# Memory keys and values in three rounded passes, and the queries in the same block

## The reference, cut to what matters

```python
mem_k_p = mem_prompt @ xa_wk        # (256, 1024) @ (1024, 1024): keys of the memory, an output too
mem_v_p = mem_prompt @ xa_wv        # values of the memory, an output too
q = h @ xa_wq                       # (1056, 1024) @ (1024, 1024): queries
s = q @ k^T * 256**-0.5             # per head of 256
o = softmax(s) @ v
```

## Time and profile before

| what | us |
|---|---|
| median of three runs | 1609.36 (1607.07 to 1612.99) |
| the profiled execution | 1610.8 |
| its span, first to last instruction | 1608.8 |
| memory stage, first product to last (L2410) | 776.4 to 836.4 |
| queries, first pass to last | 844.0 to 939.3 |

### The profile page before, as it was taken

The page is one execution under the profiler, slowest core; times in us unless marked ns, Lnnn a source line. Parts: engine busy times, 40 slices in busy tenths (PEclk is TensorE's granted clock), DMA queues, the critical chain, the costliest instruction groups (busy, mean ns, idle before and its releaser), DMA issues. The chain is left out here.

```text
span 1608.8 us, 24942 instructions
## 1 busy us (share of the span) xinstructions
PE 1353.9 (84%) x9823; PEld 942.6 (59%) x9824; DVE 735.0 (46%) x1154; ACT 425.5 (26%) x897; POOL 189.1 (12%) x188
## 2 busy tenths in 40 slices
PE   5997999689987988799879989979951998999930
PEld 3665999655556886587439978768721333433310
DVE  4333464357755653676211013356545443444429
ACT  1213234168763321411111134332110111111110
POOL 0000000014327620000000000000000111111042
PEclk9998999789998995899899999989975999999975
DMA  9111121130003000300631025230074496792256
GB/s 330 45 54 40 40 55 50 38 90 17 1 4 120 4 4 15 134 1 1 235 105 40 14 105 211 104 138 1 1 288 172 147 352 221 287 338 78 74 164 216
DMA packets 79139, 174.32 MB, mean 108 GB/s; under 512 B 13076, under 2 KB 44955, under 8 KB 72627
## 3 DMA queue, kind: packets, MB, share of 16 engines
q1 hardware_dynamic: 69579, 137.73, 24.4%
q0 software_dynamic: 5856, 21.24, 4.3%
q10 hardware_dynamic: 3600, 13.90, 2.2%
HBM read 142.27 MB, written 30.66 MB: 107 GB/s over the span
## 5 line engine op out<-in xcount | busy, mean ns | idle before, releaser
L3071 PE MATMUL bank<-arena,hT 128*64 x384 | 172.9, 604 | 11.3 <-DVE hT L3180 4.9
L3072 PE MATMUL bank<-arena,hT 128*64 128x512 f32 x384 | 172.9, 604 | 0.0
L3071 PEld LDWEIGHTS bank<-arena,hT 128*64 128x64 f32 x384 | 53.3, 140 | 123.6 <-issue 123.6
L3191 DVE COPY arena<-arena 128x4096 f32 x24 | 55.1, 2295 | 130.3 <-PE bank L3072 118.3
L498 PE MATMUL bank<-arena,hT 128*128 128x344 f32 x384 | 114.4, 458 | 0.0
L498 PEld LDWEIGHTS bank<-arena,hT 128*128 128x128 f32 x384 | 73.5, 193 | 37.3 <-issue 1.4
L2146 PE MATMUL bank<-hT_rest,f_w_high 128*128 128x352 f32 x288 | 93.4, 324 | 0.0
L3039 POOL DMA_INDIRECT hT<-tokens,row_token x24 | 40.3, 1679 | 441.7 <-PE bank L3056 228.7
L3095 PE MATMUL bank<-arena,hT 128*64 x192 | 87.5, 599 | 2.4 <-ACT hT L3135 2.4
L3097 PE MATMUL bank<-arena,hT 128*64 128x512 f32 x192 | 87.5, 599 | 0.0
L1614 PE MATMUL bank<-arena 64*64 64x64 f32 (+1 forms) x1920 | 69.1, 224 | 3.5 <-DVE arena L1987 3.0
(11 more groups left out here) (490 smaller groups left out, 2946.7 us busy)
## 6 DMA issues: line engine op xcount, KB each, us to landing
arena<-in_ex_wg_dram SPq DMA_DIRECT2D x16, 1024.0 KB, 8.6
arena<-in_ex_wu_dram SPq DMA_DIRECT2D x16, 1024.0 KB, 10.9
arena<-in_ex_wd_dram SPq DMA_DIRECT2D x16, 1024.0 KB, 13.2
expert_rows<-hT ACTq DMA_DIRECT2D x24, 512.0 KB, 4.8
arena<-in_cache_mem_k_dram SPq DMA_DIRECT2D x8, 1024.0 KB, 5.0
arena<-in_w_in_dram SPq DMA_DIRECT2D x12, 512.0 KB, 4.0
h<-in_x_prompt_dram SPq DMA_DIRECT2D x8, 512.0 KB, 8.0
tokens<-h SPq DMA_DIRECT2D x8, 512.0 KB, 2.7
```

The costliest lines, as they stand in the source:

```text
L3071: nc.tensor.matmul(ps[UPB[u % 2]][0:LR, :], xT[:, u % 2, k, 0:LR], gate_up_of[:, bass.ds(slot, 1), :, k, :].rearrange("p a g f -> p (a g) ...
L3072: last = nc.tensor.matmul(ps[UPB[u % 2]][LR:P, :], xT[:, u % 2, k, LR:P], wB_gate_up[:, :, k, :], start=(k == 0), stop=(k == KC - 1))
L3191: nc.vector.tensor_copy(wB[:, 0:2 * EW], c.xw[:, bass.ds(e & 3, 1), 0:2 * EW].rearrange("p a n -> p (a n)")).then_inc(copied_up, 1)
```

## The change

`stage_memory` and `stage_queries` become one block, `stage_memory_and_queries`, so the engines no longer meet between them. The memory's products become `three_passes`: the turned memory is split into `memT_high` (ACT) and `memT_low` (DVE), and the weights come as eight pieces of 1 MB (512 columns of four `k`) in three slots; each piece is rounded by ACT into its own space and its rest is written by DVE over the raw piece. A piece `p` is loaded again into its slot when piece `p - 3` has been used (`done`). Each piece serves both groups of memory rows, so a bank's sum over eight `k` runs over two pieces. `load_memory_first` now loads `mem_prompt` and three pieces. SP issues the store of `Km` after the last piece's load and ahead of the query chunks, and the store of `Vm` behind the first four chunks; the waits for them stand at the end of the joint block, and a wait for the `Km` store stands on ACT ahead of the first copy into `qXT`.

```diff
 def place_memory(c):
     c.place(start=0, KT=KC * NMEM, Vm=2 * D, qXT=KC * TOK)
-    c.place(start=4096, Km=2 * D, mem=2 * D, memT=KC * NMEM, halves=3 * KC * 512)
+    c.place(start=2 * D, mem=2 * D)
+    c.place(start=4096, Km=2 * D, memTh=KC * NMEM, memTl=KC * NMEM, mR0=2048, mH0=2048, mR1=2048, mH1=2048, mR2=2048, mH2=2048)
+
+def load_memory_piece(c, sp, p):
+    src = c.T[('xa_wk', 'xa_wv')[p // 4]][0].rearrange("(k p) n -> p k n", p=P)
+    half, kh = p // 2 % 2, p % 2
+    n = (p + 2) % 3
+    sp.dma_start(c.A(f"mR{n}").rearrange("p (k n) -> p k n", k=4), src[:, 4 * kh:4 * kh + 4, half * 512:(half + 1) * 512])\
+        .then_inc(c.piece_in[n], 16)
 
 def load_memory_first(c, sp):
...
-    w = c.A("halves").rearrange("p (s k n) -> p s k n", s=3, k=KC)
-    sp.dma_start(w[:, 0], c.T['xa_wk'][0].rearrange("(k p) n -> p k n", p=P)[:, :, 0:512]).then_inc(c.half_in[0], 16)
+    for p in range(3):
+        load_memory_piece(c, sp, p)
...
         def _(sp):
-            for n in range(1, 4):
-                if n == 3:
-                    sp.wait_ge(prod, 2)
-                src = T[('xa_wk', 'xa_wv')[n // 2]][0].rearrange("(k p) n -> p k n", p=P)
-                sp.dma_start(w[:, n % 3], src[:, :, (n % 2) * 512:(n % 2 + 1) * 512]).then_inc(w_in[n % 3], 16)
-            sp.wait_ge(prod, 4)
-            for n in range(4):
-                load_query_chunk(c, sp, n)
-            for n, (name, t) in enumerate((('mem_k_prompt', Km), ('mem_v_prompt', Vm))):
-                sp.wait_ge(out_ok, 4 * (n + 1))
-                sp.dma_start(O[name][0, 0].rearrange("(m p) h d -> p m (h d)", p=P), t).then_inc(stored, 16)
-            sp.wait_ge(stored, 32)
+            for p in range(3, NP):
+                sp.wait_ge(done, p - 2)
+                load_memory_piece(c, sp, p)
+            sp.wait_ge(out_ok, 4)
+            sp.dma_start(O['mem_k_prompt'][0, 0].rearrange("(m p) h d -> p m (h d)", p=P), Km).then_inc(stored_k, 16)
+            sp.wait_ge(done, 6)
+            for n in range(4):
+                load_query_chunk(c, sp, n)
+            sp.wait_ge(out_ok, 8)
+            sp.dma_start(O['mem_v_prompt'][0, 0].rearrange("(m p) h d -> p m (h d)", p=P), Vm).then_inc(stored_v, 16)
+            for n in range(4, KC):
+                sp.wait_ge(q_prod, GRP * (n - 3))
+                load_query_chunk(c, sp, n)
+            sp.wait_ge(stored_k, 16)
+            sp.wait_ge(stored_v, 16)
 
         def _(pe):
-            pe.wait_ge(mT_ok, 4)
-            for u in range(8):
-                half, m = u // 2, u % 2
-                pe.wait_ge(w_in[half % 3], 16 * (half // 3 + 1))
-                if u >= 4:
-                    pe.wait_ge(out_ok, u - 3)
-                for k in range(KC):
-                    last = nc.tensor.matmul(ps[4 + u % 4][:, :], memT[:, k, m * P:(m + 1) * P], w[:, half % 3, k, :],
-                                            start=(k == 0), stop=(k == KC - 1))
+            def products(p):
+                half, kh = p // 2, p % 2
+                pe.wait_ge(wl_ok, p + 1)
+                if half >= 2 and kh == 0:
+                    pe.wait_ge(out_ok, 2 * (half - 1))
+                for m in range(2):
+                    for k in range(4):
+                        kk = 4 * kh + k
+                        if p < 2 and m == 0 and k % 2 == 0:
+                            pe.wait_ge(Tl_ok, kk // 2 + 1)
+                        t = slice(m * P, (m + 1) * P)
+                        last = three_passes(nc, ps[4 + 2 * (half % 2) + m][:, :], memT_high[:, kk, t], memT_low[:, kk, t],
+                                            w_high[slot(p)][:, k, :], w_low[slot(p)][:, k, :], kk == 0, kk == KC - 1)
+                last.then_inc(done, 1)
+            for p in range(NP):
+                products(p)
+                if p == 4:
+                    pe.wait_ge(out_ok, 4)
+                    for f in range(4):
+                        turns(Km, f, kturned)
+            pe.wait_ge(kT_ok, 4)
             for n in range(KC):
-                pe.wait_ge(low_ok, n + 1)
+                pe.wait_ge(ql_ok, n + 1)
...
         def _(act):
+            w_highs(0)
+            for f in range(4):
+                act.wait_ge(turned, f + 1)
+                nc.scalar.copy(memT_high[:, 2 * f:2 * f + 2, :], ps[f][:, :].rearrange("p (k m) -> p k m", k=2)).then_inc(Th_ok, 1)
+            for p in range(1, 6):
+                w_highs(p)
+            w_highs(6)
...
+            w_highs(7)
+            act.wait_ge(done, 7)
+            for n in range(3):
+                round_chunk(n)
+            act.wait_ge(stored_k, 16)
...
         def _(dve):
+            w_lows(0)
+            for f in range(4):
+                dve.wait_ge(Th_ok, f + 1)
+                nc.vector.tensor_tensor(memT_low[:, 2 * f:2 * f + 2, :], ps[f][:, :].rearrange("p (k m) -> p k m", k=2),
+                                        memT_high[:, 2 * f:2 * f + 2, :].bitcast(F32), ALU.subtract).then_inc(Tl_ok, 1)
+            for p in range(1, 3):
+                w_lows(p)
+            for half in range(3):
+                outs(half)
+                for p in (2 * half + 3, 2 * half + 4):
+                    if p < NP:
+                        w_lows(p)
+            for n in range(3):
+                chunk_low(n)
+            outs(3)
+            for n in range(3, KC):
+                chunk_low(n)
```

More of the change, by code:

```diff
@@ L2192, in stage_residual @@
         place_memory(c)
-        c.mem_in, c.half_in = s("mem"), [s(f"half{n}") for n in range(3)]
+        c.mem_in, c.piece_in = s("mem"), [s(f"piece{n}") for n in range(3)]
     w_in = c.w_out_in if split else [s(f"w{n}") for n in range(4)]
@@ L2435, in stage_queries @@
-def stage_queries(c):
-    nc, T = c.nc, c.T
+    fold = lambda x: x.rearrange("p (k m) -> p k m", k=KC)
+    memT_high, memT_low = fold(c.rounded("m_T_high", "memTh")), fold(c.rounded("m_T_low", "memTl"))
+    piece = lambda x: x.rearrange("p (k n) -> p k n", k=4)
+    w_raw = [piece(c.A(f"mR{n}")) for n in range(3)]
+    w_low = [piece(c.rounded(f"m_w_low{n}", f"mR{n}")) for n in range(3)]
+    w_high = [piece(c.rounded(f"m_w_high{n}", f"mH{n}")) for n in range(3)]
+    c.KT, c.Vm = KT, Vm
+    c.place(start=c.at["mR1"][0], qring=4 * KC * P, qhigh=4 * KC * P)
@@ L2443, in stage_queries, with slot @@
     ps = c.ps
-    s = lambda n: c.sem(f"q_{n}")
-    w_in, prod, evac, high_ok, low_ok = c.q_in, s("prod"), s("evac"), s("high"), s("low")
+    s = lambda n: c.sem(f"m_{n}")
+    mem_in, w_in = c.mem_in, c.piece_in
+    c.q_in = [s(f"q{n}") for n in range(4)]
+    turned, Th_ok, Tl_ok, wh_ok, wl_ok, done, out_ok, kturned, kT_ok, stored_k, stored_v = (
+        s("turned"), s("Th"), s("Tl"), s("wh"), s("wl"), s("done"), s("out"), s("kturned"), s("kT"), s("storedk"), s("storedv"))
+    q_prod, q_evac, qh_ok, ql_ok = s("qprod"), s("qevac"), s("qhigh"), s("qlow")
+    NP = 8
+    def slot(p):
+        return (p + 2) % 3
     with nc.Block() as block:
@@ L2464, in _, with w_highs, round_chunk @@
                                             c.hT_high[:, k, t], c.hT_low[:, k, t], k == 0, k == KC - 1)
-                    last.then_inc(prod, 1)
+                    last.then_inc(q_prod, 1)
+        @block.scalar
+        def _(act):
+            def w_highs(p):
+                act.wait_ge(w_in[slot(p)], 16 * (p // 3 + 1))
+                if p >= 3:
+                    act.wait_ge(done, p - 2)
+                nc.scalar.copy(w_high[slot(p)], w_raw[slot(p)]).then_inc(wh_ok, 1)
+            def round_chunk(n):
+                act.wait_ge(c.q_in[n % 4], 16 * (n // 4 + 1))
+                nc.scalar.copy(high[:, n % 4], ring[:, n % 4]).then_inc(qh_ok, 1)
+            w_highs(0)
[5 more added lines that the diff above has]
+            w_highs(6)
+            for f in range(4):
+                act.wait_ge(kturned, f + 1)
+                nc.scalar.copy(KT[:, 2 * f:2 * f + 2, :], ps[f][:, :].rearrange("p (k m) -> p k m", k=2)).then_inc(kT_ok, 1)
+            w_highs(7)
[3 more added lines that the diff above has]
+            act.wait_ge(stored_k, 16)
+            for n in range(KC):
+                for u in range(GRP * n, GRP * (n + 1)):
+                    act.wait_ge(q_prod, u + 1)
+                    nc.scalar.copy(qXT[:, n, (u % GRP) * GT:(u % GRP + 1) * GT], ps[u % 8][:, 0:GT]).then_inc(q_evac, 1)
+                if n + 3 < KC:
+                    round_chunk(n + 3)
@@ L2467, in _, with w_lows @@
         @block.vector
         def _(dve):
[L2469 to L2486 removed]
+            def w_lows(p):
+                dve.wait_ge(wh_ok, p + 1)
+                nc.vector.tensor_tensor(w_low[slot(p)], w_raw[slot(p)], w_high[slot(p)].bitcast(F32), ALU.subtract).then_inc(wl_ok, 1)
@@ new lines, in outs, with chunk_low @@
+            def outs(half):
+                dst = (Km, Vm)[half // 2]
+                dve.wait_ge(done, 2 * half + 2)
+                for m in range(2):
```

(5 more changed lines are left out.)

74 lines of the change are left out of this document (11 added, 63 removed).

## The result

The changed kernel takes **1589.05 us** (median of four runs, 1582.56 to 1591.17), the kernel before 1610.59 in the same comparison (1607.07 to 1612.99). The ratio is 0.9862 with a 95% interval of 0.9844 to 0.9880: 21.5 us less by the medians, where 21.6 were forecast, and 1589.05 where 1587.8 was. The profiled execution of after took 1591.17 us with a span of 1589.2; of before 1610.8 and 1608.8.

A forecast was written before the change was run, and what follows sets the result against it. PE was taken to bound memory and queries as one chain with a hole and slow start; 11.2 + 1.2 - 0.7 + 9.9 = 21.6 us less gives 1587.8 us, own range 1584.5 to 1592, reaching on to 1598.

The forecast's parts named there:

- The products: Memory stage on PE: 64 plain float32 products, 54.8 us, become 192 passes of 0.227 us, 43.6 us; gain 11.2 us.
- The turn of Km: Transposes of Km in the memory stage: a piece's products cover the wait for DVE's copy, 1.97 us left; gain 1.2 us.
- The start: Memory's first product waits for cast and subtractions, coming at 777.1 instead of 776.40; loss 0.7 us, half clock kept at 2.0.
- The feed: Load, cast and subtraction of a memory piece, 9.5 to 9.9 us, fit under two pieces' 10.9 us; cost nothing.
- The seam: Between memory and queries: PE goes on without a stop at full clock, 1.7 us to spare; gain 9.9 us.
- The late feed: Memory pieces 3 to 6 come late after a 14.0 us landing, 13.5 us in all: 1601.3 us; chance 0.12.
- open seam: Before the queries PE stops for a late chunk 0 and starts at half clock, 9.9 us back: 1597.7; chance 0.07.
- the gain reached the end: Denies the rival that later stages start no earlier although 21 us are won: 1609.4; chance 0.05.
- The rival of the clock: Memory products: PE waits long for every refilled piece and runs its 192 passes at 1.2 GHz: 1629.4; chance 0.04.
- The sum: Whole kernel: the gains and the loss make 21.6 us less, for a median of 1587.8 us.

The follow-up runs named there:

- control: The changed kernel with no edit, run again on the second chip: 1587.92 us, 0.9859 of the kernel before.

## Why the prediction was right, step by step

**The products** came as priced. The passes of after start 0.227 us apart at full clock (110 spacings from 782.67 to 807.64), as in stage `o`: the price of an operation read from another stage of the same program, with the same shape and the same weight loads, carried over without a correction. From the first product to the first query pass it is 47.16 us, where the forecast's 43.6 of passes, 2.0 of half clock and 1.97 of turn make 47.6.

**The turn of Km** has no pause before it and lasts 1.91 us, so the cover by a piece's products held.

**The start** was forecast at 5.0 us from the first turn to the first product (772.08 to 777.1) and took 4.95 (773.86 to 778.81). The wait that ended last is the one named, the subtraction of the first quarter of the turned memory (`m_T_low`, L2518). Piece 0 was in time. The half clock that I kept at 2.0 us was there in after (3.6 us at 0.50, 1.8 us of work), but it is not a fixed price: of the six profiles here of kernels with this start, one was without it (the last section has more).

**The feed** was the step that could fail, with 1.0 us of slack. The casts and subtractions of after (ACT, L2471; DVE, L2503) show it closely:

```profile
765.24 21.43 SPq L2176 DMA_DIRECT2D arena<-in_xa_wk_dram  x4
791.74 16.69 SPq L2176 DMA_DIRECT2D arena<-in_xa_wv_dram  x4
...
791.33 1.91 ACT L2471 CAST m_w_high<-arena 128x2048 fp32r<-128x2048 f32 x1 [9.61 <-DMA arena<-in_xa_wk_dram]
...
793.28 2.29 DVE L2503 TENSOR_TENSOR m_w_low<-arena,m_w_high 128x2048 fp32r<-128x2048 f32 x1 [0.24 <-ACT m_w_high L2471]
```

The last of the four issues of keys, piece 3, ends at 765.24 + 21.43 = 786.67, so it stands near 786.3. Its cast waits for the load until 791.33, and its rest is ready at 795.57: a chain of 9.3 us, forecast 9.5 to 9.9. PE's first passes with pieces 3 and 4, the 73rd and the 97th, and the subtraction of piece 4:

```profile
796.99 0.39 PE L2145 MATMUL bank<-m_w_high,m_T_high 128*128 128x512 f32 x1
798.89 2.29 DVE L2503 TENSOR_TENSOR m_w_low<-arena,m_w_high 128x2048 fp32r<-128x2048 f32 x1 [3.32 <-ACT m_w_high L2471]
802.43 0.39 PE L2145 MATMUL bank<-m_w_high,m_T_high 128*128 128x512 f32 x1
```

The margin is 1.4 us for piece 3 and, the least of all, 1.2 us for piece 4 (ready at 801.18). The casts of all five refilled pieces were released by their load, and none of PE's passes behind the first by a subtraction. The experiments bound it from both sides: with two passes PE waits for pieces, and with a ring of two it waits four times. Of the combinations that were run only three passes with three slots hides the feed.

**The seam** closed fully. The cast of chunk 0 was released not by its load but by PE's end of piece 6:

```profile
820.73 2.01 ACT L2475 CAST q_w_high<-arena 128x1024 fp32r<-128x1024 f32 x2 [4.41 <-PE bank L2147]
...
821.82 3.50 DVE L2513 TENSOR_TENSOR q_w_low<-arena,q_w_high 128x1024 fp32r<-128x1024 f32 x3 [3.04 <-ACT q_w_high L2475]
```

Its subtraction is done at 821.82 + 3.50 / 3 = 823.0 and PE comes at 825.97, 3.0 us later. The forecast had taken the longest landing as the last wait and 1.7 us of margin; the landing was earlier, and the order of the waits was the other way round, at no cost. The store of `Vm`, issued at 827.49, now runs beside the query passes. Cutting the block again brought the 9.9 us back as 10.3. The block began 1.78 us later than in before; less these, the forecast's points are met within 0.5 us: first product at 777.0 (forecast 777.1), first query pass at 824.2 (824.7), end of the queries at 917.1 (917).

**The rivals.** The late feed and the open seam did not come about, and the gain reached the end: what follows the queries took 0.7 us more. The open seam's price held (10.3 us for 9.9). The late feed's did not hold as it was priced: the prediction gave it pauses alone (13.5 us) and kept the clock for a rival of its own, but with two slots the pauses of 11.3 us came together with a falling clock and cost 18.2. The rival of the clock was right that a late feed brings the clock down, and wrong in the point from which it decides: the prediction let it begin at pauses as long as the seam's 7.54 us, and with two slots it fell behind pauses of 3.96, 3.89 and 2.19 us. It was right, too, that not all passes would run slowly (some 10 us at half clock, as slow as before and not 20 us slower), but its reason, that a ring of three catches up at half clock, was not put to the test: with the ring of two the clock was back at 1.00 by 797.5, 814.4 and 831.4, with PE at work, and the next pause came all the same. So the safety of the change was smaller than I had said: a landing of 14 us was not needed, but by an estimate one some 3.5 to 5 us longer than now (the margin of 1.2 to 1.4 us and a pause of 2.2 to 4.0 us, though a pause of 2.20 us in the kernel with two passes was not followed by a fall). The Trainium skill, page "TensorE: Matmul & The Clock Gate", section "Loop structure matters more than you think", has the rule that the prediction weighed, cold matmuls where each batch waits for its transfer. The kernel with two slots agrees with it by its 0.50 to 0.55 behind three of its four waits, and the kernel with two passes, whose clock was at 1.00 behind its longest wait, 2.20 us, shows that such waits need not bring it about. This did not move the forecast, since after has no pause behind its first product.

**The sum** was 21.6 us; the medians give 21.5, and from the block's first turn to the end of the queries the profiles give 22.1: 12.86 for products and turn (forecast 12.4), 0.63 lost at the start (0.7), 9.85 at the seam with the clock behind it (9.9). So the parts were right and not only their sum. The agreement of the medians to 0.1 us is partly luck: the four runs of before lie 5.9 us apart, those of after 8.6.

## What to carry to other kernels

Before products are made cheaper, write down the chain that feeds one ring slot (load, cast, subtraction, with a duration from a row for each) beside the time that the slots ahead of it last at the new price; here 9.3 us against 10.9, and with a third fewer passes or a slot less PE waited for the feed. Price an operation by the same shape elsewhere in the program's own trace, at full clock. A block's end into which PE ran cost its pause (7.5 and 8.3 us here) and then the half clock behind it (4.8 and 6.0 us); a join of two blocks is worth looking for wherever the next block's first operands can be there in time.

## What the runs showed of the hardware that was not expected

- **Length of a pause alone does not decide whether the clock falls.** Behind 2.20 us (two passes, at 793.72) the granted clock stayed at 1.00; behind 2.19 us (two slots, at 826.72) it went to 0.50. In the kernel with two slots it was still at 1.00 for the first passes behind the pause and fell while PE was working again (starts 0.23 us apart from 827.06 to 827.98, then 0.41 and more). At the seam of before it fell within the pause: 1.00 from 836.4 to 838, 0.50 from 840 on. What PE did before differs between the two places, these are one profile of each kernel, and no run here separates what decides.
- **The same code can meet the clock at different levels.** The start of the memory stage is the same in after, its control, and the kernel with PE's wait at the seam; the clock there was at 0.50 over the first products in the first two and at 1.00 from 774 on in the third. So 2 us of a start can come or go from one execution to the next, and a single profile of a kernel that is meant to repair it shows nothing.
- **The clock and the time of a run go together.** Of the four runs of after the shortest, 1582.56 us, has a mean granted clock of 0.924, the others, 1588.58 to 1591.17, have 0.915 to 0.917. The control shows it again: 1581.80 at 0.922, the others, 1586.65 to 1590.95, at 0.915 to 0.919.
